# Order of the attention's projections, and 6 gathered rows placed elsewhere, in a one-core encoder block

## The reference, cut to what matters

```python
h = rms_norm(x, g_mix[layer]);  proj = h @ w_in[layer]        # columns: pool 256 | q 768 | k 768 | v 768
pool_out = multiscale_pool(p, w_pool[layer], pool_scale[layer])
for gi, (window, dilation) in enumerate(((128, 1), (512, 4), (2048, 16))):   # 4 heads of 64 each
    o, lse = dilated_window_attention(q[:, :, hs], k[:, :, hs], v[:, :, hs], window, dilation, slopes[hs])
x = x + concatenate([pool_out, attn * softmax(lse over the three)]) @ w_out[layer]
# expert FFN: 8 retrieval heads, 16 experts of 16384 each, per token
q = (ht @ w_q).reshape(PEER_CHUNK, PEER_HEADS, 2, PEER_HALF);  s = q . subkeys;  top 16 of each half, top 16 of the sums
act = gelu(einsum('thkd,td->thk', u[expert], ht));  out = einsum('thk,thkd->td', (gate * act), v[expert])
x = rms_norm(x + out, g_final)
```

## Time and profile before

| | us |
|---|---|
| median of 3 runs | 2577.65 |
| lowest, highest | 2576.46, 2580.89 |
| the profiled execution, its own time | 2577.02 |
| its span | 2575.0 |
| PE busy | 2513.7 |
| DVE busy | 2116.4 |
| POOL busy | 1509.7 |
| ACT busy | 879.8 |

### The profile page before, as it was taken

How to read it: one execution, slowest core, us unless ns; L and a number is a source line. 1 busy time by engine, 2 the same in 40 slices (tenths; PEclk the granted TensorE clock), 3 DMA queues, 4 the chain that set the end, 5 groups by cost and what they waited for, 6 DMA issues and landing times.

```text
span 2575.0 us, 41533 instructions
## 1 busy us (share of the span) xinstructions
PE 2513.7 (98%) x15177; PEld 2247.5 (87%) x15177; DVE 2116.4 (82%) x4504; ACT 879.8 (34%) x1658; POOL 1509.7 (59%) x1046
## 2 busy tenths in 40 slices
PE   8999989999999999998999999998999999999998
PEld 6777768999999999998999999987888888888887
DVE  7022273699999999999999997789998999989998
ACT  4223252322222222234777773232222222222222
POOL 2111030346777778886666668856665676666663
PEclk9999999999999999998999999999999999999999
DMA  4110022337899999998999999999999999999995
GB/s 155 49 33 25 26 89 99 123 111 233 308 337 335 351 330 357 347 341 304 395 398 394 400 401 410 400 380 377 381 375 380 367 379 379 376 379 369 377 374 212
DMA packets 296672, 763.35 MB, mean 296 GB/s; under 512 B 25824, under 2 KB 116320, under 8 KB 293728
## 3 DMA queue, kind: packets, MB, share of 16 engines
q0 software_dynamic: 110592, 402.70, 41.7%
q1 hardware_dynamic: 161280, 288.81, 31.9%
q10 hardware_dynamic: 24672, 70.33, 7.1%
HBM read 669.47 MB, written 92.27 MB: 296 GB/s over the span
## 4 chain that ended last, share of the span: by engine, by line
PE 66%; DVE 12%; POOL 4%; DMA 3%; issue 1%; ACT 1%; SPq 0%; another core or an unknown queue 0%; DVEq 0%; ACTq 0%
PE bank L1793 25%; PE bank L2199 19%; PE wide L2199 13%; DVE u_row L1469 5%; PE bank L2167 3%; PE bank L2020 3%; PE bank L2077 2%; POOL w_lo L718 2%; POOL u_row L735 2%; DMA g_first<-g_d 1%; DVE rest_k L1436 1%; DVE ix L1439 1%; POOL u_row L730 1%; DVE ix L1442 1%; DMA u_row<-in_u_rows,ids 1%
## 5 line engine op out<-in xcount | busy, mean ns | idle before, releaser
L786 POOL DMA_INDIRECT d_row<-in_v,ids x330 | 564.2, 1710 | 297.0 <-DVE yg L1691 225.2
L1793 PE MATMUL bank<-h_hi,w_hi 128*128 128x320 f32 (+1 forms) x2368 | 557.1, 316 | 8.6 <-POOL w_lo L718 7.9
L1793 PE MATMUL bank<-h_hi,w_lo 128*128 128x320 f32 (+1 forms) x2368 | 546.5, 312 | 0.0
L1793 PE MATMUL bank<-h_lo,w_hi 128*128 128x320 f32 (+1 forms) x2368 | 546.3, 312 | 0.1
L718 POOL TENSOR_TENSOR w_lo<-w_raw,w_hi 128x512 fp32r<-128x512 f32 (+1 forms) x230 | 367.1, 1614 | 178.3 <-DVE gate_j L1611 95.4
L730 POOL DMA_INDIRECT u_row<-in_u_rows,ids x384 | 403.7, 1051 | 110.9 <-issue 82.2
L1469 DVE CUSTOM_DVE_ANT_0 u_row<-wide,u_row 128x1024 f32<-128x1024 f32 x384 | 449.6, 1220 | 10.3 <-DMA u_row<-in_u_rows,ids 6.2
L1691 DVE SCALAR_TENSOR_TENSOR yg<-d_row,uh,yg 128x1024 f32<-128x1024 f32 x330 | 409.8, 1277 | 1.5
L1793 PEld LDWEIGHTS bank<-h_hi,w_hi 128*128 128x128 f32 x2368 | 395.4, 189 | 14.4 <-POOL w_lo L718 7.5
L1793 PEld LDWEIGHTS bank<-h_lo,w_hi 128*128 128x128 f32 x2368 | 399.2, 189 | 2.9 <-issue 0.4
L1793 PEld LDWEIGHTS bank<-h_hi,w_lo 128*128 128x128 f32 x2368 | 398.7, 189 | 2.5
(11 more groups left out here) (234 smaller groups left out, 4131.1 us busy)
## 6 DMA issues: line engine op xcount, KB each, us to landing
w_raw<-in_u SPq DMA_DIRECT2D x128, 512.0 KB
v_raw<-in_v ACTq DMA_DIRECT2D x126, 512.0 KB
act_d<-act_st SPq DMA_DIRECT2D x128, 320.0 KB
g_d<-g_st SPq DMA_DIRECT2D x20, 2048.0 KB
a_raw<-act_d SPq DMA_DIRECT2D x154, 256.0 KB
g_raw<-g_d SPq DMA_DIRECT2D x120, 256.0 KB
w_raw<-in_w_q SPq DMA_DIRECT2D x32, 512.0 KB
w_raw<-in_w_in SPq DMA_DIRECT2D x20, 512.0 KB
```

The source lines that it names most:

```text
L786: nc.gpsimd.indirect_dma_start(d_row[k % DR][:, :], None, v_rows, bass.IndirectOffsetOnAxis(ids[:, c:c + 1], 0)).then_inc(d_in[k % DR], 16)
L1793: ins = pe.matmul(banks[h][:, 0:n], lhs[:, part], rhs[:, k, h * n:(h + 1) * n], start=(k == 0 and lhs is lhs_hi and rhs is h_hi), stop=(k ...
```

## The change

Three edits in one.

1. **Projections.** A group's steps are written out in a list `STEPS`: first the 8 halves of the 4 value banks, then the 16 halves of queries and keys, with the turned tiles spread between those banks (tile j follows bank m when `tiles * m // 8 <= j < tiles * (m + 1) // 8`). The pieces of `w_in` are loaded in the order values, queries, keys (`V_FIRST`), so the values are pieces 2 + 6g and 3 + 6g. Group 0 is projected by the same steps, with the pooling matmuls after step 17 (values, three banks of queries, three turned tiles). Group 1's lead of two halves (now one value bank) is moved ahead of `qk(0, 0)`. The work for the next group is allotted over 15 units, by a cost of 8 for a half and 1 for a turned tile; unit 15 has none.
2. **Dots.** `TILE_DOTS` ends in 3 instead of 4, so `ROWS_FRONT` and `ROWS_C` are smaller by 5, and the last columns of u come later.
3. **Early rows.** `EARLY` is 24 instead of 27: 48 early rows instead of 54, and 336 late ones instead of 330. Six of the 14 middle groups of stage 3 (the last six of them) add 22 rows instead of 21, one more in unit 7.

```diff
-TILE_DOTS = (3, 3, 3, 3, 3, 3, 3, 4)
+TILE_DOTS = (3, 3, 3, 3, 3, 3, 3, 3)
-EARLY = 27
+EARLY = 24
 ROWS_UNIT = (2, 2, 2, 2, 2, 3, 2, 2, 2, 2)
+ROWS_UNIT_MORE = (2, 2, 2, 2, 2, 3, 2, 3, 2, 2)
+MORE_GROUPS = 6
-    by_group = [ROWS_UNIT0, *[ROWS_UNIT] * (NG - 2), ROWS_UNIT_LAST]
+    by_group = [ROWS_UNIT0, *[ROWS_UNIT] * (NG - 2 - MORE_GROUPS), *[ROWS_UNIT_MORE] * MORE_GROUPS, ROWS_UNIT_LAST]
...
+        V_FIRST = (4, 5, 0, 1, 2, 3)
+        STEPS = []
         for g in range(GROUPS):
-            for _ in range(4):
-                banks += 2
-                PIECE_BANKS.append(banks)
+            tiles = len(turned_tiles(g))
+            steps = [("v", m, half) for m in range(4) for half in range(2)]
             banks += 4
             PIECE_BANKS += [banks] * 2
             PJ_VT.append(banks)
-            banks += len(turned_tiles(g))
+            for m in range(8):
+                steps += [("p", m, half) for half in range(2)]
+                banks += 1
+                if m % 2:
+                    PIECE_BANKS.append(banks)
+                turned = range(tiles * m // 8, tiles * (m + 1) // 8)
+                steps += [("t", j, 1) for j in turned]
+                banks += len(turned)
+            STEPS.append(steps)
             PJ_G.append(banks)
...
-        HALVES, BUSY_UNITS = 24, 12
+        BUSY_UNITS, LEAD, POOL_AT = 15, 2, 17
         def steps_by(g, k):
-            tiles, lead = len(turned_tiles(g)), 2 if g == 1 else 0
-            if k < BUSY_UNITS:
-                return lead + ((HALVES - lead) * (k + 1) + BUSY_UNITS - 1) // BUSY_UNITS
-            return HALVES + min((k - BUSY_UNITS + 1) * (tiles + 2) // 3, tiles)
+            lead, cost = LEAD if g == 1 else 0, [1 if kind == "t" else 8 for kind, _, _ in STEPS[g]]
+            upto = sum(cost[:lead]) + (sum(cost[lead:]) * min(k + 1, BUSY_UNITS) + BUSY_UNITS - 1) // BUSY_UNITS
+            return next(n for n in range(lead, len(cost) + 1) if sum(cost[:n]) >= upto)
...
-                load_piece(n, win_d[n])
+                load_piece(n, win_d[2 + (n - 2) // 6 * 6 + V_FIRST[(n - 2) % 6]])
...
+                for kind, m, half in STEPS[g]:
+                    if kind == "v":
...
+                        if m == 3:
+                            for n in (4 + 6 * g, 5 + 6 * g):
+                                upper_slot(n, n)
+                    elif kind == "p":
+                        q, hf, n = m // 2, m % 2, 4 + 6 * g + m // 2
...
+                        if hf and n + 2 < IN_PIECES:
                             upper_slot(n + 2, n + 2)
...
-            for k in range(4):
-                project(2 + k)
+            projection_steps(0, 0, POOL_AT)
...
-            projection_steps(0, 16, HALVES + len(turned_tiles(0)))
+            projection_steps(0, POOL_AT, len(STEPS[0]))
             pe.wait_ge(pool_ev, 4)
...
+            projection_steps(1, 0, LEAD)
             pe.wait_ge(pj_free, PJ_G[0])
             qk(0, 0)
             asked = 1
-            projection_steps(1, 0, steps_by(1, -1))
```

More of the change, by code:

```diff
@@ L474, in build @@
         PJ_ALL = PIECE_BANKS[-1]
-        HALVES, BUSY_UNITS = 24, 12
+        BUSY_UNITS, LEAD, POOL_AT = 15, 2, 17
         def steps_by(g, k):
-            tiles, lead = len(turned_tiles(g)), 2 if g == 1 else 0
-            if k < BUSY_UNITS:
-                return lead + ((HALVES - lead) * (k + 1) + BUSY_UNITS - 1) // BUSY_UNITS
-            return HALVES + min((k - BUSY_UNITS + 1) * (tiles + 2) // 3, tiles)
+            lead, cost = LEAD if g == 1 else 0, [1 if kind == "t" else 8 for kind, _, _ in STEPS[g]]
+            upto = sum(cost[:lead]) + (sum(cost[lead:]) * min(k + 1, BUSY_UNITS) + BUSY_UNITS - 1) // BUSY_UNITS
+            return next(n for n in range(lead, len(cost) + 1) if sum(cost[:n]) >= upto)
         def parts_by(g, k):
-            steps = steps_by(g, k)
-            return min(steps, HALVES) // 2 + max(steps - HALVES, 0)
+            return sum(half for _, _, half in STEPS[g][:steps_by(g, k)])
         def v_turned(g, c):
@@ L905, in projections @@
                     act.wait_ge(pv_done, UNITS)
-                for q in range(4):
-                    n = 2 + 6 * g + q
-                    dst = (qt if q < 2 else kt)[g % 2][:, q % 2, :].rearrange("p (r l) -> p r l", r=n_res)
-                    for hf in range(2):
+                for kind, m, half in STEPS[g]:
+                    if not half:
+                        continue
+                    if kind == "v":
+                        dst = v_turned(g, m % 2).rearrange("p (r l) -> p r l", r=n_res)
+                        take(dst[:, :, m // 2 * length // 2:(m // 2 + 1) * length // 2],
+                             lambda b: b[:, :].rearrange("p (l r) -> p r l", r=n_res))
+                        if m == 3:
[3 more added lines that the diff above has]
+                        q, hf, n = m // 2, m % 2, 4 + 6 * g + m // 2
+                        dst = (qt if q < 2 else kt)[g % 2][:, q % 2, :].rearrange("p (r l) -> p r l", r=n_res)
                         take(dst[:, :, hf * length // 2:(hf + 1) * length // 2],
@@ L936, in _ @@
                     if k or g == 1:
-                        for _ in range(parts_by(g, k - 1) - (parts_by(g, k - 2) if k > (g != 1) else 0)):
+                        for _ in range(parts_by(g, k - 1) - (parts_by(g, k - 2) if k else 0)):
                             next(work, None)
@@ L1869, in project_v @@
             def project_v(g, m, half):
-                n, c, hf = 6 + 6 * g, m % 2, m // 2
+                n, c, hf = 2 + 6 * g, m % 2, m // 2
                 b = pj[0]
@@ L1900, in projection_steps @@
             def projection_steps(g, s0, s1):
-                for s in range(s0, s1):
-                    m, half = divmod(s, 2)
-                    if s >= HALVES:
-                        turn_v(g, s - HALVES)
-                    elif m < 8:
-                        project_half(2 + 6 * g + m // 2, m % 2, half)
+                for kind, m, half in STEPS[g][s0:s1]:
+                    if kind == "t":
+                        turn_v(g, m)
+                    elif kind == "p":
+                        project_half(4 + 6 * g + m // 2, m % 2, half)
                     else:
-                        project_v(g, m - 8, half)
+                        project_v(g, m, half)
             def qk(g, k):
@@ L2002, in _ @@
                 if g + 1 < GROUPS:
-                    projection_steps(g + 1, steps_by(g + 1, k - 1) if k or g == 0 else 0, steps_by(g + 1, k))
+                    projection_steps(g + 1, steps_by(g + 1, k - 1), steps_by(g + 1, k))
                 m = n - (GROUPS - 1) * UNITS - 2
```

23 lines of the change are left out of this document (3 added, 20 removed).

## The result

| | before | after |
|---|---|---|
| median, us (runs beside each other, 4 and 4) | 2577.9 | 2610.78 |
| lowest, highest | 2576.46, 2580.89 | 2606.78, 2613.99 |
| profiled execution, and its span | 2577.02, 2575.0 | 2613.99, 2612.0 |
| mean granted clock over the span | 0.993 | 0.990 |

A forecast was written before the change was run, and what follows sets the result against it. PE was taken as the bound, busy 2513.7 of 2575.0 us. Edit 1 +23.7, edit 2 -6.6 and edit 3 0 gave +17.1 us on 2577.0, plus 0.6 for the median: 2594.7 us, range 2583 to 2606.

The forecast's parts named there:

- Edit 1, waits: Stage 1: the new order adds 20.7 us of PE waits and removes 7.2 us of old ones.
- the handovers: Stage 1, after each group's last value bank: PE waits 4.2 us for the first query piece, three times, 12.6 us.
- Edit 1, clock and breaks: Stage 1: three clock falls behind the 4.2 us waits cost 7.8 us, broken runs of halves 2.4 us.
- the rival of more clock falls: Stage 1: shorter pairs of waits drop the clock too, up to two more falls, +5.2 us, 2599.9; chance 0.14.
- Edit 2 = -6.6: Stage 2: PE's 4.0 us wait for the routing tables goes, with its clock fall of 2.6 us.
- POOL asks for one row fewer early in the tiles, so some of the 7.9 us may go too: Stage 2: PE's waits for lowered chunks of u, 7.9 us, may shrink; edit 2 at most 8.7 us in all.
- Edit 3: 0: Stage 3: the row added in six groups is hidden behind PE, 0 us; upper bound 8.4 us.
- The handover was not hidden: Rival, stage 1: new pieces are ready when the last value bank ends, so the change is faster, 2571.5; chance 0.06.
- the clock did not hold: Rival, stage 1: waits as computed but no clock fall after them, 7.8 us less, 2586.9; chance 0.12.
- stage 3 did not pay the 8.4 us: Rival, stage 3: the moved rows cost transfer time, at most 8.4 us, 2603.1; chance 0.05.
- The dots bring nothing: Rival, stage 2: PE meets DVE as before, 4.01 us wait and clock fall included, 2601.3; chance 0.09.

The follow-up runs named there:

- e7: Kernel before with edit 1, value banks filled first halves first and ACT told so, to write the first query piece earlier: 2583.73 us, 0.9993.
- e15: Kernel before (25 dots per tile) with POOL's asks for rows one row earlier in the dense tiles (+ 6 instead of + 5): one run, 2589.67 us.
- e2: Kernel before with edits 2 and 3 alone, projections as before: 2584.33 us, 1.0022.
- e3: Kernel before with edit 2 alone (24 dots per dense tile, 54 early rows as before): 2593.87 us, 1.0053.
- e4: Kernel before with edit 3 alone (48 early rows, 25 dots per dense tile as before): 2582.18 us, 1.0005.
- e5: Kernel before with edits 2 and 3, and POOL's asks one row later in the dense tiles (margin 4 instead of 5): 2583.02 us, 0.9992.
- e12: Kernel before with edits 2 and 3, and POOL's asks two rows later in the dense tiles (margin 3 instead of 5): 2578.3 us, 0.9991.

## Why the prediction was too low, point by point

- **Edit 1, waits: right.** Added 20.7 forecast; measured 3 x 4.05 at the handovers, 1.75 (1.9), 0.88 (0.9), 1.88 before the first `turn` (1.9), and 1.29, 1.18, 0.31, 0.61 at the ends of the groups (3.4), together 20.05. All waits of stage 1 behind PE's first projection went from 10.8 to 23.8 us, +13.0 against 20.7 - 7.2 = 13.5. That the handover is the cause is shown by e7, which takes the waits for the pieces away and leaves the other new ones.
- **Edit 1, clock and breaks: right in sum, off in kind.** 24.3 - 13.0 leaves 11.3 us; the forecast had 7.8 + 2.4. How much of it each of the two took was not measured. Five falls instead of three: the rival of more clock falls came true, beside the forecast and not in its stead. The argument against it, that 212 to 226 us held 1.00 through 3.2 us of idle time in small pieces, rested on one execution. In e15, whose projections are those of before, the same four waits were followed by 6.8 us at the lower level:

```profile
226.90:233.70 6.80, 6.65 (x24) 4.51 (x25) 1.54 (x7) 1.08 (x6) 0.00 (x0) 0.50 0.00 0
```

- **Edit 2: the step that failed.** "Edit 2 = -6.6" ("That wait goes, and with it its clock fall"), from five dots less and the wait for the routing tables. The wait did go, in after, e2 and e3, and the way from the tiles to stage 3 is 7.0 us shorter. That the dots did it is less sure: it went in e4 too, with all 25 dots. And `route_done` has only four of the five dots fewer ahead of it, 4.9 us and not 6.1; the copies behind it have all five. But the step took every other instruction of the tiles to last as long as before. DVE's steps with two SBUF operands lost 37.4 us to POOL's lowering in e3, against 17.3, and the tiles grew by 13.2 us. Edit 2 alone cost 0.53% (0.37 to 0.70), 13.7 us, 8.4 of it the wait at stage 3 that edit 3 removes; in its company (e2) it cost 5.7 us, where the bounds were -8.7 and 0. No bound above zero was given. The sign that it could be otherwise stood in the trace of before: the subtraction in `route` takes 836 ns in one tile, shown above, and 286 with no lowering beside it.
- **"POOL asks for one row fewer early in the tiles, so some of the 7.9 us may go too"**: the opposite; those waits became 22.1 us. DVE, longer in its tiles, uses rows later, POOL stands behind its asks, and the chunk behind the ask comes late to PE. The longest wait, 3.7 us at 1174.9, came another way: ACT stood 8.1 us behind DVE's `route`, and split the chunk only then.
- **Edit 3: 0 was right alone** (1.0005), and for the two edits together: 56 rows ahead of stage 3 instead of 57. By itself it gave back 9 us (e3 to e2), because edit 2 alone puts 62 there and PE then waits for DVE. The added rows may show as one PE wait of some 1.1 us in stage 3 (last line of the first list of waits): of the eleven traces with these rows three have it (after, e5, e12), of the seven without none. Here are 300 us of the middle groups (columns as in the earlier trace rows): DVE is 6.6 us busier than there, PE 1.1 us less, and the transfers have room.

```profile
2200.00:2500.00 300.00, 298.89 (x1319) 247.25 (x1318) 274.45 (x296) 77.15 (x100) 215.69 (x121) 1.00 1.04 380
```

- **The rivals.** The handover was not hidden; the clock did not hold; stage 3 did not pay the 8.4 us. "The dots bring nothing" was nearest in kind, and too mild: it had no mechanism that makes them harm.

With what the runs give, edit 1 +0.83%, edits 2 and 3 +0.22%, the sum is 1.05%, against 1.23% (1.01 to 1.45) measured.

## What to carry to other kernels

When work is moved between slots, look at what the old order hid: a load, split and lowering of 4 us was free for as long as PE had tiles to turn, and became three bare waits plus their clock falls when weights were needed at once; splitting the handover (first halves first) mended it for the price of one semaphore. When one engine's list is shortened, don't take the rest of the list at its old durations if its steps share a port with another engine: look at the spread of one shape's duration in the trace before (291 to 1058 ns for `route` in the kernel before) and put the far end of it into the range. And test such an edit at several places and rates: 24 dots cost 13 us of tile time with the gap in one place and nothing with it in another, which in its turn kept a wait further on. Where a rival leans on a clock that held, look at a second execution: this one's didn't hold.
